# Tile 0's head 6 moved from VectorE's additions to TensorE's, and forgetting heads' scores in pairs, in a one-core attention and expert-retrieval kernel

## The reference, cut to what matters

```python
def body(xb):                                   # 128 tokens
    q = (xb @ w_q).reshape(128, 8, 2, 128)      # 8 heads, 2 halves
    sc = einsum('thpd,hpkd->thpk', q, sub_keys) # 2 x 128 scores
    # top 16 of each half, top 16 of their 256 sums -> eidx, gate g
    u_sel = take(u_tab, eidx, axis=0)           # (128, 8, 16, 1024)
    hid = gelu(einsum('thkd,td->thk', u_sel, xb)) * g
    v_sel = take(v_tab, eidx, axis=0)
    return einsum('thk,thkd->td', hid, v_sel)
```

## Time and profile before

| what | us |
|---|---|
| median of 3 runs | 1541.17 (1539.67 to 1543.49) |
| profiled execution | 1541.62 |
| its span, first to last instruction | 1539.8 |
| TensorE busy | 1269.3 (82%) |
| VectorE busy | 1077.6 (70%) |
| ScalarE busy | 459.8 (30%) |
| GpSimd busy | 751.5 (49%) |
| DMA moved | 596.50 MB, mean 387 GB/s |

### The profile page before, as it was taken

How to read it: one execution, slowest core, us unless ns; L and a number is a source line. 1 busy time by engine, 2 the same in 40 slices (tenths; PEclk the granted TensorE clock), 3 DMA queues, 4 the chain that set the end, 5 groups by cost and what they waited for, 6 DMA issues and landing times.

```text
span 1539.8 us, 13062 instructions
## 1 busy us (share of the span) xinstructions
PE 1269.3 (82%) x3727; PEld 658.2 (43%) x3727; DVE 1077.6 (70%) x2520; ACT 459.8 (30%) x1200; POOL 751.5 (49%) x637
## 2 busy tenths in 40 slices
PE   9999999988888488999787777677886787777778
PEld 7766655665545234444333333233332233332333
DVE  3247699999988867566666676666666766666654
ACT  3432355466343022222222222221222222222212
POOL 0016477675667443454544554445444554444440
PEclk9999999999989699999899999989999999999998
DMA  9669799997999999999999999999999999999995
GB/s 382 250 250 413 275 330 351 370 376 268 340 371 392 391 421 416 421 421 421 421 422 422 421 422 421 421 422 421 422 421 421 422 422 421 422 420 422 421 421 208
DMA packets 99741, 596.50 MB, mean 387 GB/s; under 512 B 11480, under 2 KB 11480, under 8 KB 42328
## 3 DMA queue, kind: packets, MB, share of 16 engines
q0 software_dynamic: 89856, 536.91, 86.0%
q1 hardware_dynamic: 9816, 58.77, 9.6%
HBM read 593.54 MB, written 2.10 MB: 387 GB/s over the span
## 4 chain that ended last, share of the span: by engine, by line
DMA 42%; PE 15%; DVE 6%; POOL 3%; issue 2%; ACT 2%; DVEq 0%; POOLq 0%
PE acc L994 13%; DMA map_mem<-in_peer_uv_dram,eidx 10%; DMA w_ring<-in_peer_uv_dram,eidx 9%; DMA v_all<-in_peer_uv_dram,eidx 7%; DMA act_mem<-in_peer_uv_dram,eidx 6%; DMA v_ring<-in_peer_uv_dram,eidx 3%; DMA mix_mem<-in_peer_uv_dram,eidx 3%; DMA u_ring<-in_peer_uv_dram,eidx 3%; DMA v_ring<-in_peer_v_dram,eidx 2%; PE mm L786 1%; ACT diag L1228 1%; DVE map_mem L1549 1%; DVE w_ring L1549 1%; PE sc L786 1%; POOL v_ring L692 1%
## 5 line engine op out<-in xcount | busy, mean ns | idle before, releaser
L1220 ACT ACTIVATE gel<-hid 128x4 f32<-128x4 f32 x126 | 25.8, 205 | 722.2 <-DVE hid L1549 712.5
L685 POOL DMA_INDIRECT u_ring<-in_peer_u_dram,eidx x112 | 136.8, 1221 | 172.9 <-DVE eidx L1529 99.5
L994 PE MATMUL acc<-v_all,diag 128*128 128x512 f32 x256 | 129.2, 651 | 61.1 <-ACT diag L1228 60.6
L692 POOL DMA_INDIRECT v_ring<-in_peer_v_dram,eidx x112 | 133.4, 1192 | 66.4 <-DVE h L1577 38.0
L1577 DVE SCALAR_TENSOR_TENSOR h<-v_ring,coef,h 128x1024 f32<-128x1024 f32 x112 | 143.9, 1284 | 14.3 <-DMA v_ring<-in_peer_v_dram,eidx 11.3
L994 PE MATMUL acc<-map_mem,diag 128*128 128x512 f32 x248 | 123.3, 644 | 32.0 <-ACT diag L1228 32.0
L994 PE MATMUL acc<-v_ring,diag 128*128 128x512 f32 x248 | 120.1, 629 | 32.3 <-ACT diag L1228 28.7
L1541 DVE CUSTOM_DVE_ANT_0 u_ring<-u_ring,hn 128x1024 f32<-128x1024 f32 x112 | 136.6, 1220 | 14.2 <-DMA u_ring<-in_peer_u_dram,eidx 14.0
L994 PE MATMUL acc<-u_ring,diag 128*128 128x512 f32 x248 | 119.1, 626 | 27.4 <-ACT diag L1228 25.8
L1228 ACT ACTIVATE diag<-ident,coef 128x128 f32<-128x128 f32 x392 | 126.3, 390 | 39.1 <-DVE coef L1567 30.8
L711 POOL DMA_INDIRECT v_all<-in_peer_uv_dram,eidx x64 | 76.1, 1189 | 92.3 <-PE acc L994 81.7
(11 more groups left out here) (281 smaller groups left out, 2331.9 us busy)
## 6 DMA issues: line engine op xcount, KB each, us to landing
w_ring<-in_slabs_dram SPq DMA_DIRECT2D x29, 1024.0 KB, 8.4
v_ring<-in_slabs_dram SPq DMA_DIRECT2D x6, 1024.0 KB, 11.2
u_ring<-in_slabs_dram SPq DMA_DIRECT2D x6, 1024.0 KB, 10.9
map_mem<-in_slabs_dram SPq DMA_DIRECT2D x6, 1024.0 KB, 7.9
h<-in_x_dram SPq DMA_DIRECT2D x4, 512.0 KB, 12.5
u_ring<-in_peer_u_dram,eidx POOLq DMA_INDIRECT x112, 6.9
v_ring<-in_peer_v_dram,eidx POOLq DMA_INDIRECT x112, 7.1
v_all<-in_x_cols_dram SPq DMA_DIRECT2D x3, 512.0 KB, 7.4
```

Source lines behind the costliest of these rows:

```text
L685: nc.gpsimd.indirect_dma_start(out=u_ring[:, c % U_RING, :], out_offset=None, in_=peer_u[0], in_offset=bass.IndirectOffsetOnAxis(ap=eidx[n ...
L692: nc.gpsimd.indirect_dma_start(out=v_ring[:, c % V_RING, :], out_offset=None, in_=peer_v[0], in_offset=bass.IndirectOffsetOnAxis(ap=eidx[n ...
L994: last = nc.tensor.matmul(acc[half][:, :], diag[:, c % COLS, :], v_row(n, c)[:, half * BANK:(half + 1) * BANK], start=first, stop=(n % PH ...
L1220: nc.scalar.activation(gel[:, par, g0:g0 + COLS], hid[:, par, g0:g0 + COLS], ACT.Gelu).then_inc(gelu_done, 1)
```

## The change

1. `HOST_HEADS` goes from 7 to 6. Six heads of tile 0 are hosted, in 216 slots; the pieces, which are the same, are spread over slots 0 to 207. Heads 6 and 7 of tile 0 come as rows of 8 KB.
2. Head 7's key scores are now still to be searched when the first rows of 8 KB are asked for, so their memory in `store` is no longer a free place. It becomes the last of the ten (place 9) and its first gather waits for the 10th step of head 7's search. `FREE_ROWS` is 5.
3. `pair_scores` makes the scores of forgetting heads m and m + 1 together, at even steps: both 64-partition matmuls, then both 40-partition ones. It waits for the banks of both. Odd steps make none.

```diff
-HOST_HEADS = 7
+HOST_HEADS = 6
...
-        row_mem += [store[:, 0:PH * 2 * K1], mix_mem[:, :]]
+        row_mem += [mix_mem[:, :]]
         FREE_ROWS = len(row_mem)
         row_mem += [m for flat in (ur_flat, vr_flat) for m in halves_of(flat)]
+        row_mem += [store[:, 0:PH * 2 * K1]]
         RING = len(row_mem)
...
+        TK_FIRST = 10
...
+                elif place == RING - 1:
+                    pool.wait_ge(topk_step, TK * (PH - 1) + TK_FIRST)
...
+            def pair_scores(g, step):
+
+                t, first = at_step(g, 0, step)
+                nk, j = P * (t + 1), GROUPS[g].index(t)
+                if first == 0:
+                    pe.wait_ge(selq_ready, 2 * (t + 1))
+                both = [(HD * (m % 2), m // 2, map_no[(t, m)]) for m in (first, first + 1)]
+                for lo, ch, k in both:
+                    if k >= len(sc_b):
+                        pe.wait_ge(sc_drained, k + 1 - len(sc_b))
+                    nc.tensor.matmul(sc_b[k % len(sc_b)][:, 0:nk], qT[lo:lo + HD, ch, j * P:(j + 1) * P], kv_t[lo:lo + HD, ch, 0:nk],
+                                     start=True, stop=False)
+                for lo, ch, k in both:
+                    nc.tensor.matmul(sc_b[k % len(sc_b)][:, 0:nk], selq[lo:lo + 40, ch, t % 2, :], caug[lo:lo + 40, 0:nk],
+                                     start=False, stop=True).then_inc(sc_full, 1)
+
             def scores(g, half, step):
-                if at_step(g, half, step):
+                if half == 0:
+                    if step % 2 == 0 and at_step(g, half, step):
+                        pair_scores(g, step)
+                elif at_step(g, half, step):
                     t, it = at_step(g, half, step)
...
```

15 lines of the change are left out of this document (3 added, 12 removed).

## The result

The changed kernel takes 1563.43 us (median of 4 runs, 1560.33 to 1564.16) against 1541.78 us (median of 4) before: 1.0134 times as long, 95% interval 1.0117 to 1.0152. It is slower, as forecast, but by 21.7 us and not by 5.8; 1563.4 lies above the range, which ended at 1557. The profiled execution took 1563.66 us, its span is 1561.9.

What follows compares the result with a forecast made beforehand. Row transfers bound the kernel from about 540 us, VectorE mostly the hosted heads; hosted stage -33.3 us and row stage +39.9 make +6.6, taken as +5.8: 1547.0 us, range 1536 to 1557.

Steps and rivals of the forecast that it cites:

- forget (start): Tile 0's forgetting heads, before 105 us, TensorE-bound: three pairs save 0 to 3.4 us, taken as 1.8 us.
- stretch 2: Tiles 1 to 3's forgetting heads, 199 to 330 us: VectorE the longer at 121 us, 9.9 us shorter less 1 us.
- stretch 3: Differential heads, 78 us: 3.1 rows and some search less leave VectorE 69 us, so 9.1 us shorter.
- stretch 4: Output projection and queries, 95 us: 3.6 rows and half a search less, 10 us shorter, between 8.6 and 11.7.
- last dot to first row matmul: Change of stages, 503 to 545 us, with one free place less: between -2.5 and +2.5 us, taken as 0.
- The price of a row behind: Row stage, bound by transfers: 2.49 us for each moved row, 39.9 us more for 16 rows.
- stretch 1: Up to the first forgetting step: TensorE's projections set the pace, first map of tile 1 comes 3.5 us earlier.
- What pairs save: Forgetting heads' scores on TensorE: 2.0 us a tile 3 pair against 3.84; 16.4 us saved, leaving 112 to 117 us.
- less whatever two nearly full engines cost each other: Forgetting heads' stretch: mutual cost of nearly full VectorE and TensorE, taken as 1 us off the 9.9 us gain.
- rival (d): Forgetting heads: pairs stall for score banks emptied by VectorE, 12 us lost, 1559 us; chance 0.08, half of it another 0.03.
- Rival (c): 195 to 408 us: TensorE, not VectorE, sets the pace, so pairing's saving comes whole; faster, 1536 us; chance 0.15.
- The chance I gave to slower: Whole kernel slower by over 0.3%: chance 0.51, against 0.34 for within and 0.15 for faster.

Runs made afterwards that it cites:

- the two other kernels on after's plan: Before with paired scores and pieces pressed into slots 0 to 207: 1570.91 us; after without the second differential map in tiles 1 to 3's turned sum: 1563.09 us.
- its one shifted one: The kernel before with every piece from slot 100 on two slots later: 1546.6 us, 1.0032 times before.
- the three shifted kernels: After with every piece from slot 100 on one, two or five slots later: 1558.87, 1557.45 and 1558.53 us.
- the cheaper dots at seven heads: The kernel before, single scores, with each hosted dot product over 512 of its 1024 columns: 1525.28 us, 0.9895 times before.
- the dense kernel with seven heads: The kernel before with paired scores and its pieces pressed into slots 0 to 207: 1570.91 us, 1.0188 times before.
- the only two kernels with all of the computation that beat the one before: Before with pairs, `LATE_HEADS` 5, first eight projections at 1.3 times their share: 1535.85 us; the same, pieces from slot 100 two slots later: 1537.89 us.

## Why the prediction was right or wrong

Marks, in us, with what the step gave:

| | before | after | change | predicted |
|---|---|---|---|---|
| forget (start) | 173.24 | 171.12 | -2.1 | -1.8 |
| first map of tile 1 | 199.07 | 193.57 | -3.4 more | -3.5 |
| stretch 2 | 131.0 | 128.0 | -3.0 | -9.9 + 1.0 |
| stretch 3 | 78.6 | 79.3 | +0.7 | -9.1 |
| stretch 4 | 92.9 | 79.7 | -13.2 | -10.0 |
| last dot to first row matmul | 20.5 | 22.2 | +1.7 | 0 |
| first row matmul to end | 1017.8 | 1059.2 | +41.4 | +39.9 |

The changes sum to +22.1, the difference of the spans.

**The price of a row behind** was nearly right: 41.4 us for 16 rows at 421 to 422 GB/s. The 1.7 us ahead of them lie at the change of stages, where rows of both kinds share the queue: 387 GB/s from 485 to 530, against 396 in the same 45 us of before, 506 to 551. Where the 1.5 above 39.9 lie isn't shown.

**Start and stretch 1** were right, the start in part by luck (with after's plan the forget piece came at 171.1 to 172.8 us, and after's own execution is the earliest), and so was the reason: VectorE's wait for the forget piece grew from 6.85 to 15.08 us, and less TensorE work brought that piece 8.7 us earlier. How much of the 2.1 us at the start is the pairs' is not settled: forget came 3.3 us earlier for them with six heads, 0.6 with seven.

**What pairs save** was right per pair (1.92 us against 2.0), and what TensorE then needs in stretch 2 was too (111.3 to 117.7 us busy in the kernels with pairs, six heads and whole projections, 112 to 117 predicted). As busy time in stretch 2 it came to 9.4 us and not 16.4, since part of the work ran at 1.2 GHz behind waits (granted clock 0.92 against 0.97).

**The step that failed** is the length of stretches 2 and 3: "less whatever two nearly full engines cost each other; I take 1 us for that", and in stretch 3 no such term. I took the longer of two sums, VectorE's, as the length, and put the waits that come with it at 1 us and at nothing. That sum did fall (by 12.0 us in stretch 2 against 9.9, by 7.6 in stretch 3 against 9.1), but 9.3 and 8.5 us came back as waits (4.7 to 14.0, 1.9 to 10.4). The two terms missed by 5.9 and 9.8 us, 15.7 together; stretch 4, 3.2 us better, and the last two rows of the table, 3.2 worse, cancel. (With the stretch 2 of the two other kernels on after's plan, 125 us, the first miss is 2.9; the total time doesn't follow it, since one of them, at after's 1563 us, has 3.7 us more in stretch 4.) How much of these 15.7 us is the plan of slots can be bounded only:

- Up to 11 are the **slots** into which the same pieces fall. Before's plan is better by 5.2 us than its one shifted one, after's worse by 4.6 to 6.0 than its three. With both moved by two slots the kernels take 1546.6 and 1557.45 us: the change costs 10.9 us and not 21.7 (10 by the two ratios to before), and the first row matmul comes 527.58 - 495.72 = 31.9 us earlier, where the sum had 33.3. Stretch 3, 84.3 against 75.2, is then 9.1 us shorter, the predicted figure, though the stretch holds 2.3 us of other work in the one. But this pair of plans is the best of after's and the worse of before's. Against before's own plan, from which the prediction set out, the three shifted kernels cost 15 to 16 us (before took 1542.76 beside them), so that 5 to 7 of the 15.7 are after's bad plan and 9 to 11 stay. That the change also makes a new plan was in my sum only through the marks; I held the length between two marks to be a matter of work.
- At the plans moved by two slots the rest is about 5 us, between 10.9 and the forecast 5.8. 3.0 of it lie in the row stage (1060.0 against 1017.1 us from the first row matmul on, 42.9 and not 39.9), 1.4 ahead of it, and 0.8 in what I had taken off the sum.

The mechanism: a map of scores goes from TensorE (scores) to VectorE (mask), ScalarE (exponential), TensorE (turn) and ScalarE again (the copy out of the bank), each in a fixed order with its other work between. Where a long piece stands ahead of a hand-over, the next engine waits unless it has rows to fill the time, and once it has waited, TensorE waits behind it and loses clock. With six heads, stretch 2 took 128.0 us with sums of 113.0 and 117.7, 120.1 with 95.9 and 113.6, and 116.3 with 90.1 and 111.3: 10.3, 6.5 and 5.0 us above the longer sum; before stood 3.9 above it. This term belongs to no engine, and the view of busy times doesn't show it.

**The rivals.** The sign that I had given for rival (d) came, 14.0 us of VectorE's waits for TensorE, but (d) was not the reason: TensorE waited 1.0 us for a score bank, and without pairs the kernel is 9.6 us slower. The sign could not tell (d) from hand-overs. The Trainium skill's rule that stood beside (d), "TensorEngine Tiling (Array Packing)", Performance Considerations (tiling speeds up TensorE but not the emptying of PSUM), fits what the pairs did at seven heads: TensorE had 8.6 us less to do and its waits for banks grew from 5.0 to 16.7 us. But it was not the score banks (3.5 us, before 3.0), which (d) had in mind; it was the bank of turned maps, which ScalarE empties (9.5 us, before 2.0), and the one of the values (3.7 us). The prediction looked at VectorE's share of the emptying and left out ScalarE's. Rival (c), that TensorE sets the pace from 195 to 408, fell for stretch 3 (6.4 us less of its work gave 0.9) and was half true of before's stretch 2, as the cheaper dots at seven heads show (20.5 us gave 2.6). The chance I gave to slower, 0.51, was too small for a change whose every favourable term assumed that one engine's time is the path.

**Not settled**: which slots make a plan good. With six heads, stretch 3 took 78.4 to 80.9 us in every kernel with after's slots and whole dots (74.6 with dots over half the columns), 85.3 and 79.0 in two with other slots, and 72.0 to 77.8 in five more; I have not traced a path through them. And before's shift was tried at one distance only.

## What to carry to other kernels

Where engines hand each item round in a fixed order, the stretch is longer than its fullest engine's sum (stretch 2 here by 4 us before and by 5 to 10 of 116 to 128 in three kernels with six heads), and any change of the counts also deals out new slots, worth some 5 us in two of the kernels here and 2 in a third. So measure such a change, and the kernel before it, at two or three shifted plans before its worth is judged: at the plans given the change cost 21.7 us, at plans moved by two slots 10.9. And put the filling work where one engine rules alone: four rows more in the first stretch are part of the only two kernels with all of the computation that beat the one before (0.9974 and 0.9978).

## What was unexpected of the hardware

A faster TensorE can lower its own clock. With pairs alone its granted clock in stretch 2 fell from 0.97 to 0.91, while its waits there grew from 5.0 to 16.7 us, and of the 16.4 us that the pairs should save at 2.4 GHz 8.6 showed as less busy time.

The float32 matmuls over 64 and 40 partitions of two heads of tile 3, in separate halves, take 1.92 us where those of one head alone take 1.92: the bias matmuls over 40 partitions overlap as fully as those over 64.

Gathers of 4 KB rows don't reach the rate of 8 KB rows: 367 GB/s at a share of 0.97 in after's stretch 4, which also loads weights, and 361 at 0.95 in the dense kernel with seven heads from 481 to 550 us, where hardly anything but rows is moved; 8 KB rows move 422 at 1.01 in the row stage.
